# Four junctions of a two-block transformer on one core: last phases in threes, another order of the norm's chain, first products that take high parts by fours

## The chip, the core and the metric

One Trainium2 chip, one of its cores. The metric is the device time of one launch in microseconds, the median of several runs, for the whole network below. In the profile PE is TensorE, DVE VectorE, ACT ScalarE, POOL GpSimd, SP the queue that issues the weights' DMAs.

## What is computed

One sequence of 256 tokens, width 1024, float32. The first block has two layers, each a mixer and a SwiGLU FFN with adaptive modulation; the second block has a mixer (MoBA and gMLP), cross-attention to a memory and a PEER expert layer. What matters here is the step from one projection to the next norm, four times in the first block:

```python
mod = silu(c) @ ada_w + ada_b                       # shifts, scales, gates
y = concat(mixer outputs) @ w_out                   # or (silu(h@w_gate) * (h@w_up)) @ w_down
x = x + gate * rmsnorm(y, post_g)
h = rmsnorm(x, pre_g) * (1 + scale) + shift         # not modulated for the second block's mixer
# second mixer, from its input projection:
log_a = log_sigmoid((h @ w_glr) @ w_gk2 + b_gk) / 16
q, k = h @ w_gq, h @ w_gk                           # then GLA in chunks, v, gates, NSA
```

## The kernel before

All products in full precision are made of three: each f32 operand is cut into a high part (what the array's reduced format holds) and a low part (the rest), and high by high, high by low and low by high are summed in PSUM. Of the rows, hH and hL are high and low parts; of the weights, `whi` and `wlo`.

**Weights.** `weight_order` (L152) lists all slabs of 2048 columns in the order of their use. SP loads slab n into one of three places of `raw` once both low parts of slab n - 3 are made (L3250 to L3257). A slab has two blocks of 1024 columns. ACT makes a block's high part (`cut_hi`, L2489), and may do so as soon as the block three before it is used up, because `whi` and `wlo` are rings of three blocks. DVE, or POOL for blocks that `lo_engine` gives it, subtracts to get the low part (`cut_lo`, L1399). TensorE waits for the low part once, at a block's first tile (`tile`). How far ahead ACT and DVE cut is written into each stage (`se_cuts` and `ve_cuts`: two blocks past the last tile named). Each engine follows one list, so a cut asked for late in the list comes late.

**The modulation** of later stages is summed on DVE in pieces between other work (`ve_ada`, L1425 and L1428: two steps a piece, one 512 KB DMA each through a ring of two). After the fourth piece of a group TensorE turns the sum by eight matmuls (`pe_ada`, L742), and that call waits for the piece before it.

**A junction.** The last projection of a stage (`pe_out` for the mixers, `pe_down` 9 and 10 for the FFNs) accumulates four PSUM banks (two token tiles by two halves of the width). Its last phase takes the last two blocks (512 columns of moving operand, three products a tile) bank by bank, so that the banks end one after another. Ahead of it the gains of the gate are turned into rows (`pe_gate_rows`, L687) once DVE has made them (L1538). Then, by bank: ACT squares it (L2531), takes Ln and Exp for the root (L2542, L2544); DVE scales it (L1546) and updates x (L1555); ACT squares x and takes the root; DVE makes the unit rows (L1483); TensorE transposes them (L675), with fillers ahead so that it isn't idle (L669, L658; counts in `KEEP`). `se_junction` and `ve_junction` hold the order. From the transposes ACT makes high parts (L2603, L2601) and some shifted rows (L2607), DVE the other shifted rows (L1507) and the low parts (L1514, L1497) (`se_normed`, `ve_normed`). The first products of the next projection (`split` set) go tile by tile, and each waits for the high and the low part of its rows (`pe_split`). In the second FFN gate and up projections take high and low rows in one instruction of 512 columns (L582, `pe_linear_halves`).

**The second mixer's start** (`pe_mix1`, `ve_mix1`, `se_mix1`): w_glr, w_gqk 0, log_a (L1007), w_gqk 1 to 3. DVE adds the bias (L1919), ACT makes Abs, Exp and Ln (L2822, L2824, L2827) with two high parts between, DVE finishes (L1925, L1928) and scans (L1932). Then GLA begins (L1026).

Of the kernel before, what the change touches and what calls it, by code (L numbers as in the profile page):

```python
# [41 lines left out]
KEEP = {"ffn0": (16, 3, 8), "mix1": (16, 3, 8), "ffn1": (14, 3, 8), "mix2": (16, 3, 0), "peer": (0, 8, 0)}  # L42
# [14 lines left out]
FIRST = (("w_glr", 0, 0), ("w_mqk", 0, 0))  # L57
BY_PE = (2, 3, 6, 7)
SHIFTED_BY_ACT = (0, 2)
# [99 lines left out]
def weight_order():  # L159
# [19 lines left out]
    for name, n in (("w_glr", 1), ("w_gqk", 4), ("w_gv", 4), ("w_gg", 4), ("w_ncd", 1), ("w_nq", 2), ("cmp_w1", 2),  # L179
                    ("w_nks", 1)):  # L180
        some(name, *range(n))
# [21 lines left out]
class Weights:  # L203
# [3 lines left out]
    def __init__(self, counts, D, raw, whi, wlo, slots):  # L207
        self.counts, self.D, self.raw, self.whi, self.wlo, self.slots = counts, D, raw, whi, wlo, slots
        self.slabs = weight_order()
# [21 lines left out]
        half_slab("peer_up", 127)  # L231

# [13 lines left out]
    def lo_engine(self, j):  # L246
        name, i, half = self.blocks[j]
        if name[:6] in ("w_gate", "w_up0", "w_up1", "w_down"):
# [3 lines left out]
        return "G" if (name, i, half) in FIRST else "V"  # L252

    def parts(self, j):
# [3 lines left out]
        k = (j % NBLK) * BLK  # L258
        return w[:, half * BLK:half * BLK + cols], self.whi[:, k:k + cols], self.wlo[:, k:k + cols], ready
# [25 lines left out]
class Memory:  # L285


    def __init__(self, sb):
# [15 lines left out]
        self.hT = tiles8(self.hT_t)  # L304
        self.cs_parts, self.cs_pick = chi[0:48, 0:T], chi[0:48, T:T + 16]
# [162 lines left out]
def program(nc, D, out_dram):  # L468
    with ExitStack() as ctx:
# [21 lines left out]
        W = Weights(counts, D, m.raw, m.whi, m.wlo, [sem(f"slab_landed{k}") for k in range(NRAW)])  # L491
# [29 lines left out]
class Net:  # L521
# [70 lines left out]
    def pe_linear(self, e, name, i, kt, nn, xh, xl, split=None, eager=False, ada=True):  # L592
# [5 lines left out]
        order = [(j, k) for k in range(kt) for j in range(nn)] if split else [(j, k) for j in range(nn) for k in range(kt)]  # L598
        for n, (j, k) in enumerate(order):
            if eager and 2 * n == len(order):  # L600
                self.pe_ada(e)
            if split and j == 0:
                self.pe_split(e, split, k)
            keys = [("full", name, i)] if n == len(order) - 1 else []
            self.pe_mm3(e, ps[:, j * 256:(j + 1) * 256], self.W.tile(e, name, (i * nn + j) * kt + k), xh[:, k, :],
                        xl[:, k, :], n == 0 if split else k == 0, k == kt - 1, *keys)

    def pe_linear_halves(self, e, name, i, split=None):
# [3 lines left out]
        if split:  # L612
            for j in range(2):
                self.banks.take(e, name, i, j)
        for n in range(16):
            j, k = (n % 2, n // 2) if split else (n // 8, n % 8)
            if split and j == 0:
                self.pe_split(e, split, k)
            if not split and k == 0:
                self.banks.take(e, name, i, j)  # L620
# [86 lines left out]
    def pe_out(self, e, name, ks, xh, xl, first, last, nm, split=None, ada=True):  # L707
# [4 lines left out]
        for k in ks:  # L712
# [4 lines left out]
            if last and k >= ks[-1] - 1:  # L717
                continue
# [2782 lines left out]
```

## Time and profile before

| | us |
|---|---|
| median of 3 runs | 1981.6 (1979.27 to 1986.51) |
| the profiled execution | 1974.73 |
| its span, first to last instruction | 1972.9 |
| PE busy | 1887.3 (96%) |
| DVE busy | 1445.0 (73%) |
| ACT busy | 993.6 (50%) |
| POOL busy | 258.3 (13%) |

Busy time counts each engine's own instructions; a matmul's end is modelled, so two in a row overlap in the rows. A row of a timeline gives the start, the time, engine, line, tiles and, in brackets, how long the engine was idle before it and what released it. Rows that merge several like instructions say x2 or more; their time runs from the first start to the last end.

### The profile page before, as it was taken

The numbers are of one execution on the slowest core, as the hardware profiler recorded it, in microseconds if no ns is written. First come the engines' busy times: TensorE is split into PE (matmuls) and PEld (weight loads), VectorE is DVE, ScalarE is ACT, GpSimd is POOL, SyncE is SP. The second block draws the span as 40 slices with busy tenths as digits, with TensorE's granted clock in tenths as the row PEclk, the third lists the DMA queues.
The fourth block names the chain that finished last, engine by engine and source line by source line (L and its number), as shares of the span: only waits on it lengthen the run. The fifth ranks groups of instructions, "written<-read, shape, count | busy, mean of one in ns | idle before, by whom it ended". The sixth has DMA issues, their size and how long they took to land.

```text
span 1972.9 us, 31980 instructions
## 1 busy us (share of the span) xinstructions
PE 1887.3 (96%) x12506; PEld 1702.2 (86%) x12506; DVE 1445.0 (73%) x2618; ACT 993.6 (50%) x1442; POOL 258.3 (13%) x118
## 2 busy tenths in 40 slices
PE   6899899999989899999999899999999999999998
PEld 6887799989968788889898799999988888888886
DVE  5998775558957785557666559888878887777776
ACT  6645544455435544454555546566643334444444
POOL 0001044430001044430000175000000000000000
PEclk9999999999999999999999999999999999999999
DMA  8754476756464255546344344577767766465452
GB/s 327 246 185 151 146 269 250 260 203 225 169 233 146 99 206 188 191 151 231 137 150 171 125 153 172 191 215 215 214 209 260 299 235 232 174 235 192 176 207 108
DMA packets 94549, 391.88 MB, mean 199 GB/s; under 512 B 7680, under 2 KB 41776, under 8 KB 56000
## 3 DMA queue, kind: packets, MB, share of 16 engines
q1 hardware_dynamic: 94112, 389.58, 55.8%
q8 instruction: 100, 1.64, 0.3%
q10 hardware_dynamic: 288, 0.26, 0.1%
q14 instruction: 49, 0.40, 0.1%
HBM read 371.72 MB, written 15.73 MB: 196 GB/s over the span
## 4 chain that ended last, share of the span: by engine, by line
PE 76%; DVE 12%; ACT 3%; issue 2%; DMA 1%; POOL 0%; ACTq 0%; DVEq 0%; SPq 0%
PE ps L582 9%; PE acc L566 9%; PE acc L568 9%; PE acc L567 9%; PE ps L570 6%; PE ps L572 6%; PE ps L571 6%; PE ps L583 5%; PE acc L570 3%; PE acc L571 3%; PE acc L572 3%; DVE wlo L1399 2%; PE ps L1354 1%; PE acc L1354 1%; DVE arena L1428 1%
## 5 line engine op out<-in xcount | busy, mean ns | idle before, releaser
L2489 ACT ACTIVATE whi<-raw 128x1024 fp32r<-128x1024 f32 x557 | 588.4, 1059 | 450.2 <-PE acc L568 222.9
L1399 DVE TENSOR_TENSOR wlo<-raw,whi 128x1024 fp32r<-128x1024 f32 x461 | 560.9, 1224 | 282.0 <-ACT whi L2489 278.8
L570 PE MATMUL ps<-hpair,whi 128*128 128x256 f32 x1104 | 318.2, 288 | 10.5 <-DVE wlo L1399 6.3
L1399 POOL TENSOR_TENSOR wlo<-raw,whi 128x1024 fp32r<-128x1024 f32 x96 | 241.1, 2514 | 607.3 <-ACT whi L2489 607.0
L572 PE MATMUL ps<-hpair,wlo 128*128 128x256 f32 x1104 | 313.1, 284 | 0.0
L571 PE MATMUL ps<-hpair,whi 128*128 128x256 f32 x1104 | 313.0, 284 | 0.0
L566 PE MATMUL acc<-whi,chi 128*128 128x512 f32 x752 | 297.4, 395 | 3.5 <-DVE wlo L1399 1.9
L568 PE MATMUL acc<-wlo,chi 128*128 128x512 f32 x752 | 294.9, 392 | 0.0
L567 PE MATMUL acc<-whi,clo 128*128 128x512 f32 x752 | 294.2, 391 | 0.0
L582 PE MATMUL ps<-hpair,whi 128*128 128x512 f32 x800 | 284.8, 398 | 0.8 <-DVE hpair L1514 0.8
L570 PEld LDWEIGHTS ps<-hpair,whi 128*128 128x128 f32 x1104 | 212.4, 192 | 15.1 <-issue 4.9
L583 PE MATMUL ps<-hpair,wlo 128*128 128x256 f32 x800 | 224.5, 281 | 0.0
L571 PEld LDWEIGHTS ps<-hpair,whi 128*128 128x128 f32 x1104 | 212.5, 192 | 0.3
L572 PEld LDWEIGHTS ps<-hpair,wlo 128*128 128x128 f32 x1104 | 212.3, 192 | 0.0
L570 PE MATMUL acc<-hpair,whi 128*128 128x256 f32 x616 | 178.5, 290 | 7.2 <-ACT hpair L2603 4.2
L582 PEld LDWEIGHTS ps<-hpair,whi 128*128 128x128 f32 x800 | 150.3, 188 | 37.3 <-ACT hpair L2603 1.0
L572 PE MATMUL acc<-hpair,wlo 128*128 128x256 f32 x616 | 175.0, 284 | 0.0
L571 PE MATMUL acc<-hpair,whi 128*128 128x256 f32 x616 | 175.0, 284 | 0.0
L566 PEld LDWEIGHTS acc<-whi,chi 128*128 128x128 f32 x752 | 141.9, 189 | 35.1 <-issue 2.9
L568 PEld LDWEIGHTS acc<-wlo,chi 128*128 128x128 f32 x752 | 141.7, 188 | 31.9
L567 PEld LDWEIGHTS acc<-whi,clo 128*128 128x128 f32 x752 | 142.0, 189 | 27.4
L583 PEld LDWEIGHTS ps<-hpair,wlo 128*128 128x128 f32 x800 | 151.1, 189 | 2.5
(458 smaller groups left out, 2950.7 us busy)
## 6 DMA issues: line engine op xcount, KB each, us to landing
raw<-in_peer_down SPq DMA_DIRECT2D x64, 1024.0 KB, 4.9
raw<-in_peer_up SPq DMA_DIRECT2D x64, 1024.0 KB, 5.0
arena<-in_ada SPq DMA_DIRECT2D x80, 512.0 KB, 4.8
raw<-in_w_gate SPq DMA_DIRECT2D x22, 1024.0 KB, 4.7
raw<-in_w_up SPq DMA_DIRECT2D x22, 1024.0 KB, 4.8
raw<-in_w_down SPq DMA_DIRECT2D x22, 1024.0 KB, 4.8
arena<-spill SPq DMA_DIRECT2D x14, 1024.0 KB, 6.8
spill<-hT_t SPq DMA_DIRECT2D x22, 448.0 KB, 6.1
```

The lines of the kernel that those rows point to most:

```text
L566: e.matmul(out, xh, hi, start=start, stop=False, skip_group_check=True)
L567: e.matmul(out, xl, hi, start=False, stop=False, skip_group_check=True)
L568: i = e.matmul(out, xh, lo, start=False, stop=stop, skip_group_check=True)
L570: e.matmul(out, hi, xh, start=start, stop=False, skip_group_check=True)
L571: e.matmul(out, hi, xl, start=False, stop=False, skip_group_check=True)
L572: i = e.matmul(out, lo, xh, start=False, stop=stop, skip_group_check=True)
L582: e.matmul(ps.rearrange("p (s t) -> p s t", s=2), hi, self.m.hP[:, k], start=k == 0, stop=False, skip_group_check=True)
L583: i = e.matmul(ps[:, 0:T], lo, self.m.hH[:, k, :], start=False, stop=k == 7, skip_group_check=True)
L1354: t = e.matmul(ps[:, i * 128:(i + 1) * 128], m.oh1[:, n % 3, i * 128:(i + 1) * 128], m.oh2[n % 3][:, i * 128:(i + 1) * 128], start=True, s ...
L1399: e.tensor_tensor(out=lo, in0=w, in1=hi.bitcast(F32), op=ALU.subtract).then_inc(*X(("lo", j)))
L1428: e.scalar_tensor_tensor(out=m.ada_acc, in0=w, scalar=c, in1=m.ada_acc, op0=ALU.mult, op1=ALU.add).then_inc(*V(*([("ada", s)] if k else [])))
L2489: e.activation(hi, w, ACT.Copy, scale=1.0).then_inc(*self.A(("hi", j)))
```

## The change

- `SPARE`: the last block of w_out0b, w_down0, w_out1b and w_down1 gets a place of its own, half of `chi` and `clo`, outside the rings, so that four blocks can be live. The last phase of the four projections takes three blocks instead of two (`tail=3`; in `pe_down` the second half of call 9 moves into call 10, behind the gate rows).
- `se_junction`: the cut of a weight block moves behind the last root; one square over a whole row of the first token tile replaces two, with eps from a constant. `ve_junction`: the eps steps move to match.
- `pe_first`, for all first products: four rows' high parts, then their low parts, and the second block's low part last. `lo_engine`: that second block's low part is POOL's in `FIRST` (gate 0, gate 1, w_gqk 0, w_mqk 0), and DVE's cut inside `ve_normed` goes.
- `ve_normed`, `se_normed`: the shifted rows of pair 0 are DVE's now. `KEEP`: fewer fillers.
- Second mixer: w_gqk 0 before w_glr, log_a after w_gqk 1.

```diff
-KEEP = {"ffn0": (16, 3, 8), "mix1": (16, 3, 8), "ffn1": (14, 3, 8), "mix2": (16, 3, 0), "peer": (0, 8, 0)}
+KEEP = {"ffn0": (13, 2, 2), "mix1": (13, 2, 2), "ffn1": (12, 2, 2), "mix2": (13, 2, 0), "peer": (0, 8, 0)}
-FIRST = (("w_glr", 0, 0), ("w_mqk", 0, 0))
+FIRST = (("w_gate0", 0, 1), ("w_gqk", 0, 1), ("w_gate1", 0, 1), ("w_mqk", 0, 1))
+SPARE = {("w_out0b", 1, 1): ("used", "w_out0a"), ("w_down0", 10, 1): ("end", "mixer0", "P"),
+         ("w_out1b", 1, 1): ("used", "w_out1a"), ("w_down1", 10, 1): ("end", "mixer1", "P")}
-SHIFTED_BY_ACT = (0, 2)
+SHIFTED_BY_ACT = (2,)
...
+    def pe_first(self, e, name, i, kt, outs, starts, xh, xl, split, full):
+        nn = len(outs)
+        for k0 in range(0, kt, 4):
+            for k in range(k0, k0 + 4):
+                e.wait_ge(*self.at("hi", split, k))
+                for j in range(nn):
+                    if j == 0:
+                        hi, lo, _ = self.W.tile(e, name, i * nn * kt + k)
+                    else:
+                        b, hi = self.W.high(name, (i * nn + j) * kt + k)
+                        if k == 0:
+                            e.wait_ge(*self.at("hi", b))
+                    e.matmul(outs[j][0], hi, xh[:, k, :], start=k == 0 and j in starts, stop=False, skip_group_check=True)
+                    if j == 0:
+                        e.matmul(outs[0][0], lo, xh[:, k, :], start=False, stop=False, skip_group_check=True)
+            for k in range(k0, k0 + 4):
+                e.wait_ge(*self.at("lo", split, k))
+                for j in range(nn):
+                    t = e.matmul(outs[j][1], self.W.high(name, (i * nn + j) * kt + k)[1], xl[:, k, :], start=False,
+                                 stop=j == 0 and k == kt - 1, skip_group_check=True)
...
+        for j in range(1, nn):
+            for k in range(kt):
+                _, lo, end = self.W.tile(e, name, (i * nn + j) * kt + k)
+                t = e.matmul(outs[j][0], lo, xh[:, k, :], start=False, stop=k == kt - 1, skip_group_check=True)
...
-        for n in range(8):
-            tt, half, kk = (n // 4, n // 2 % 2, n % 2) if i == 10 else (n // 2 % 2, n % 2, n // 4)
+        order = ([(tt, half, k) for tt in range(2) for half in range(2) for k in (19, 20, 21)] if i == 10 else
+                 [(tt, half, 2 * i + kk) for kk in range(1 if i == 9 else 2) for tt in range(2) for half in range(2)])
...
     def pe_mix1(self, e):
-        self.pe_linear(e, "w_glr", 0, 8, 1, m.hH, m.hL, "mix1")
         for i in range(4):
-            self.pe_linear(e, "w_gqk", i, 8, 2, m.hH, m.hL)
+            self.pe_linear(e, "w_gqk", i, 8, 2, m.hH, m.hL, None if i else "mix1")
             if i == 0:
+                self.pe_linear(e, "w_glr", 0, 8, 1, m.hH, m.hL)
+            elif i == 1:
                 e.wait_ge(self.landed["gk2"], 16)
...
     def ve_normed(...):
         whole(1)
-        if first:
-            self.cut_lo(e, V, self.W.last(first, 0) + 1)
+        e.wait_ge(*self.at("hi", nm, 1))
+        whole(0)
         low(0)
...
     def ve_junction(...):
         self.ve_scaled(e, post, 1, 0)
-        self.ve_eps(e, norm, 0, 48)
         self.ve_scaled(e, post, 1, 1)
         self.ve_update(e, post, 1, 0)
         self.ve_update(e, post, 1, 1)
+        self.ve_eps(e, norm, 1, 48)
         self.ve_unit(e, norm, 0, self.m.x)
-        self.ve_eps(e, norm, 1, 48)
         self.ve_unit(e, norm, 1, self.m.x)
...
     def ve_mix1(...):
             self.ve_linear(e, "w_gqk", i, 8, 2, ada=i != 1)
             if i == 0:
+                self.ve_linear(e, "w_glr", 0, 8, 1)
+                e.wait_ge(*self.at("full", "w_glr", 0))
+                e.tensor_copy(m.low, self.banks.tile("w_glr", 0)[0:56, 0:T]).then_inc(*V(("out", "w_glr", 0)))
+            elif i == 1:
                 for h0 in range(0, 4, 2):     # additions, then ve_ada, ve_cuts(e, "w_gqk", 31), log_gate: as before
...
     def se_junction(...):
         self.se_acc_square(e, post, 1, 0)
-        self.cut_hi(e, self.W.last(first, 0) + 1)
-        self.se_x_square(e, norm, post, 0, 0)
+        self.se_row_square(e, norm, post, 0, 48)
         self.se_acc_square(e, post, 1, 1)
         self.se_root(e, post, 1, 56)
-        self.se_x_square(e, norm, post, 0, 1)
-        self.se_root(e, norm, 0, 48)
+        self.se_root(e, norm, 0, 48, self.m.kc("eps"))
         self.se_x_square(e, norm, post, 1, 0)
         self.se_x_square(e, norm, post, 1, 1)
         self.se_root(e, norm, 1, 48)
+        self.cut_hi(e, self.W.last(first, 0) + 1)
...
     def se_mix1(...):
+                self.se_linear(e, "w_glr", 0, 8, 1)
+            elif i == 1:
                 e.preload_act_table_set(LOG_SET)
...
                 e.activation(m.bcum, m.bcum, ACT.Exp, scale=-1.0).then_inc(*A())
-                self.se_cuts(e, "w_gqk", 31)
+                self.se_cuts(e, "w_gqk", 47)
...
     def ge_mix1(...):
-        self.cut_lo(e, self.G, self.W.last("w_glr", 0) + 2)
-        self.ge_cuts(e, "w_glr", 7)
+        self.cut_lo(e, self.G, self.W.last("w_gqk", 0) + 2)
```

## Rows read from the trace of the kernel before

**Rows 1.** The page: busy time, share of the span and instructions of each engine.

```profile
PE 1887.3 (96%) x12506; PEld 1702.2 (86%) x12506; DVE 1445.0 (73%) x2618; ACT 993.6 (50%) x1442; POOL 258.3 (13%) x118
```

**Rows 2.** Timeline, TensorE, first junction: start, us, engine, line, tiles [idle before <- releaser].

```profile
217.64 0.48 PE L566 MATMUL acc<-whi,hpair 128*128 128x512 f32 x1
...
224.09 0.50 PE L566 MATMUL acc<-whi,hpair 128*128 128x512 f32 x1 [0.73 <-DVE wlo L1399]
...
230.12 3.73 PE L669 MATMUL ps<-kc_t 128*128 128x128 f32 x32
```

**Rows 3.** Timeline, VectorE, first junction.

```profile
221.36 1.54 DVE L1428 SCALAR_TENSOR_TENSOR arena<-arena,gs_t 128x512 f32<-128x512 f32 x2 [1.52 <-DMA arena<-in_ada]
222.81 3.49 DVE L1399 TENSOR_TENSOR wlo<-raw,whi 128x1024 fp32r<-128x1024 f32 x3
```

**Rows 4.** Timeline, ScalarE, first junction.

```profile
229.69 1.06 ACT L2489 ACTIVATE whi<-raw 128x1024 fp32r<-128x1024 f32 x1
...
231.27 0.58 ACT L2531 ACTIVATE arena<-acc 128x512 f32<-128x512 f32 x1
...
237.00 1.02 ACT L2603 ACTIVATE hpair<-ps,mod_t,gs_t 128x256 fp32r<-128x256 f32 x2 [1.11 <-PE ps L675]
```

**Rows 5.** Timeline, first junction: DVE's last low part, next block's first product.

```profile
242.62 0.69 DVE L1514 TENSOR_TENSOR hpair<-hT_t,hpair 128x512 fp32r<-128x512 f32 x1 [0.16 <-ACT hpair L2603]
...
246.61 0.36 PE L570 MATMUL ps<-hpair,whi 128*128 128x256 f32 x1
```

**Rows 6.** Timeline, second junction: VectorE, TensorE, ScalarE.

```profile
426.02 0.17 DVE L1538 TENSOR_TENSOR gs_t<-mod_t,pv_t 128x8 f32<-128x8 f32 x1
...
433.95 3.73 PE L669 MATMUL ps<-kc_t 128*128 128x128 f32 x32
...
435.46 0.58 ACT L2531 ACTIVATE arena<-acc 128x512 f32<-128x512 f32 x1
...
440.77 1.02 ACT L2603 ACTIVATE hpair<-ps,mod_t,gs_t 128x256 fp32r<-128x256 f32 x2 [1.11 <-PE ps L675]
```

**Rows 7.** Timeline, TensorE, second mixer's start.

```profile
453.86 1.99 PE L1007 MATMUL acc<-arena 16*128 16x256 f32 x8
...
461.64 1.05 PE L742 MATMUL ps<-kc_t,arena 128*128 128x128 f32 x8
...
469.14 0.36 PE L570 MATMUL ps<-hpair,whi 128*128 128x256 f32 x1 [0.69 <-ACT arena L2501]
...
475.81 2.05 PE L1026 MATMUL acc<-arena 128*128 128x128 f32 x16 [0.69 <-ACT arena L2501]
```

**Rows 8.** Timeline, VectorE and ScalarE, second mixer's start.

```profile
456.87 1.54 DVE L1428 SCALAR_TENSOR_TENSOR arena<-arena,gs_t 128x512 f32<-128x512 f32 x2
...
460.88 1.15 ACT L2827 ACTIVATE arena<-arena,kc_t 128x1024 f32<-128x1024 f32 x1
...
464.19 2.44 DVE L1932 TENSOR_TENSOR_SCAN arena<-arena 128x256 f32<-128x256 f32 x4
...
467.78 2.35 DVE L1399 TENSOR_TENSOR wlo<-raw,whi 128x1024 fp32r<-128x1024 f32 x2
```

**Rows 9.** Timeline, VectorE, third junction.

```profile
671.33 1.22 DVE L1399 TENSOR_TENSOR wlo<-raw,whi 128x1024 fp32r<-128x1024 f32 x1
```

**Rows 10.** Timeline, VectorE and TensorE, fourth junction.

```profile
868.51 2.12 DVE L1876 TENSOR_TENSOR clo<-arena,chi 128x512 fp32r<-128x512 f32 x1 [0.70 <-ACT chi L2800]
...
872.02 1.09 PE L687 MATMUL ps<-kc_t,gs_t 128*128 128x128 f32 x8 [0.23 <-DVE gs_t L1538]
...
878.43 3.73 PE L669 MATMUL ps<-kc_t 128*128 128x128 f32 x32
...
892.13 1.23 DVE L1399 TENSOR_TENSOR wlo<-raw,whi 128x1024 fp32r<-128x1024 f32 x1 [2.84 <-DMA arena<-in_sin]
```

**Rows 11.** Stretches: us, PE busy (x), granted clock (1.00 is 2.4 GHz), DMA, GB/s.

```profile
554.40:558.80 4.40, 4.37 (x11) 0.50 0.89 328
```

**Rows 12.** Timeline, TensorE, first product of the experts' queries.

```profile
1128.46 0.38 PE L570 MATMUL ps<-hpair,whi 128*128 128x256 f32 x1 [1.18 <-DVE hpair L1497]
```

More of the change, by code:

```diff
@@ L178, in weight_order @@
     ffn(0)
-    for name, n in (("w_glr", 1), ("w_gqk", 4), ("w_gv", 4), ("w_gg", 4), ("w_ncd", 1), ("w_nq", 2), ("cmp_w1", 2),
+    some("w_gqk", 0)
+    some("w_glr", 0)
+    some("w_gqk", 1, 2, 3)
+    for name, n in (("w_gv", 4), ("w_gg", 4), ("w_ncd", 1), ("w_nq", 2), ("cmp_w1", 2),
                     ("w_nks", 1)):
@@ L231, in __init__ @@
         half_slab("peer_up", 127)
+        self.turn, self.owner = [], []
+        for j, key in enumerate(self.blocks):
+            self.turn.append(len(self.owner))
+            if key not in SPARE:
+                self.owner.append(j)
     def begin(self):
@@ L2534, in se_square, with se_row_square, se_root @@
         self.junk_written[k] = self.A.last
-    def se_root(self, e, nm, tt, at):
+    def se_row_square(self, e, nm, src, tt, at):
+        m = self.m
+        for half in range(2):
+            e.wait_ge(*self.at("x", src, tt, half))
+            if self.squares_made > 1:
+                e.wait_ge(*self.junk_written[half])
+        e.activation(m.junk, m.x[:, tt, :], ACT.Square, scale=1.0 / 32.0,
+                     accum_out=m.small[:, at + 2 + tt:at + 3 + tt]).then_inc(*self.A(("square", nm, tt, 1)))
+        self.junk_written = [self.A.last, self.A.last]
+    def se_root(self, e, nm, tt, at, eps=None):
         m, A = self.m, self.A
@@ L2594, in se_normed @@
             e.wait_ge(*self.at("full", nm, "turned", jj))
-            if shifts is not None and jj not in SHIFTED_BY_ACT:
+            if shifts is not None and jj in SHIFTED_BY_ACT:
+                for j in (2 * jj, 2 * jj + 1):
+                    e.activation(out[:, j, :], ps[:, (j % 2) * 256:(j % 2) * 256 + T], ACT.Identity,
+                                 bias=shifts[:, j:j + 1], scale=gains[:, j:j + 1]).then_inc(*A(("whole", nm, j)))
+            elif shifts is not None and jj:
                 e.wait_ge(*self.at("whole", nm, 2 * jj + 1))
@@ L2598, in se_normed @@
                 src = ps[:, (j % 2) * 256:(j % 2) * 256 + T]
-                last = j % 2 and shifts is not None and jj not in SHIFTED_BY_ACT
                 if shifts is None:
@@ L2603, in se_normed @@
                     e.activation(H[:, j, :], src, ACT.Identity, bias=shifts[:, j:j + 1], scale=gains[:, j:j + 1]).then_inc(
-                        *A(("hi", nm, j), *([("out", nm, "turned", jj)] if last else [])))
-            if shifts is not None and jj in SHIFTED_BY_ACT:
-                for j in (2 * jj, 2 * jj + 1):
-                    e.activation(out[:, j, :], ps[:, (j % 2) * 256:(j % 2) * 256 + T], ACT.Identity,
-                                 bias=shifts[:, j:j + 1], scale=gains[:, j:j + 1]).then_inc(
-                                     *A(("whole", nm, j), *([("out", nm, "turned", jj)] if j % 2 else [])))
+                        *A(("hi", nm, j)))
         if first:
```

104 lines of the change are left out of this document (64 added, 40 removed).

## The prediction

> **What bounds the kernel now.** I read the page first, then the engines' timelines around the four junctions (after the out-projection of either mixer and after either FFN). The page: TensorE is busy for 96% of the span [rows 1], so an edit counts by the idle time it takes from TensorE or adds to it, and by nothing else. At a junction the last product of the old projection is followed by fillers (230.12), then there is a chain ACT, DVE, TensorE up to the first high part of the normed rows (237.00), then the first products [rows 2, 4]. I call the fillers' start E and that high part's start T1. E to T1 is 6.9 us at the first junction and 6.8 at the second [rows 2, 4, 6]; by the same two views it is 6.5 at the third and 6.7 at the fourth. The prize is small. The risk sits in what feeds the stretches on either side of it: weights' low parts on DVE, and a log-gate chain after the second junction.
>
> **Last phase in threes.** No product is added. The phase that finishes the four accumulators takes 36 products (0.23 us each: 24 of them and eight small transposes fill 872.02 to 878.43 [rows 10]), so the work that may run before it shrinks by 12 products, 2.7 us. The spare block lets the high parts of the last block be made early, but what comes late is on DVE:
> - First junction. TensorE starts the projection at 217.64. Its first block takes 2.8 us, the second block's share for one accumulator 0.7, so the third block's low part is wanted at 221.1. DVE makes it at 222.8, behind a copy of modulation weights that waits for its DMA (1.52 us) [rows 3], and nothing in the change moves that. Today the same block is wanted after 24 products, and costs 0.73 [rows 2]. The third block starts at 224.09 as now, the fourth at 225.2, and 27 products follow: E at 232.1 instead of 230.1, **+2.0**, with 3.0 us of idle.
> - Second. The rows of gate gains are turned before the last phase, and want DVE's product of 426.02 [rows 6]. With one block less ahead TensorE is there at 424.9 and waits until 426.25. From there eight transposes and 36 products take 6.4 + 2.7: E at 435.3 instead of 433.95, **+1.4**.
> - Third. Low parts three and four come from DVE at 671.33 and 1.2 us later [rows 9], 0.3 and 0.5 us late for the new order: **+0.8**.
> - Fourth. The same wait is already open: the rows start at 872.02, 0.23 us after DVE's product. DVE was held by a low part of the activation that took 2.12 us [rows 10]. They can't start earlier, and 12 more products lie behind them: **+2.7**, with 3.1 us of idle before.
>
> Together +6.9. Bounds: 0, if the low parts were on time everywhere, and 12 products four times, 11.
>
> **The chain's order.** ACT no longer makes a weight block's high part inside the chain (229.69, 1.06 us) nor a square of the first half before the last accumulator's. At the first junction that square began 1.15 us after E [rows 2, 4]; now I take 0.2, the semaphore's way to an engine that is free. From it to T1 it was 5.7, and 5.3 at the second, where no GpSimd instruction ran beside the x updates (435.46 to 440.77) [rows 4, 6]. The new order has that case everywhere: GpSimd gets its block only after ACT's last root. One square over a whole row replaces two, and is done before the last accumulator. So E to T1 is 0.2 + 5.3 = 5.5: **-1.4, -1.3, -1.0, -1.2**, together -4.9. Bounds: -6 and -3, by a filler or wait of half a us at each. Fewer fillers cost nothing: 13 of 0.23 us end before the first transposes may start at E + 3.5.
>
> **First products by fours.** They may start on high parts alone, 2 us sooner. But they end with the low parts: DVE has one more pair of shifts to do, so its last low part ends 6.4 us after T1 where it ends 6.3 now (242.62 + 0.69) [rows 5]. The last four of the rows' low products and the eight with the second block's low part follow, some 8.0 after T1 instead of 8.8; then the next block waits for DVE's modulation piece and low part, 9.3 instead of 9.6 (246.61) [rows 5]. **-0.3** at the first junction, 0 at the third, within -1 and +1.
>
> The second block's low part is now GpSimd's: 2.4 us where DVE took 1.2. At the fourth junction it releases the slab that the SP queue waits for, behind which the loads of cos and sin stand; DVE waits for sin until 892.13 [rows 10] before it makes the third block's low part. That comes 1.2 us later after T1: **+1.2**, bounds 0 and 1.5.
>
> The port: the activation's low part took 2.12 us, as all do here that begin while GpSimd subtracts [rows 10]. The Trainium skill, SBUF — State Buffer, "Who interferes with whom", says that a VectorE instruction with two SBUF inputs and a GpSimd one that reads SBUF exclude each other for the whole instruction; the trace agrees. By that rule the first low part of the rows may wait some 0.3 us for GpSimd's block, 1.2 over four junctions; by the sum above, nothing.
>
> The input projection of the first stage is bound by DVE's low parts, 0. Before the experts' queries TensorE waits 1.18 us for a low part that four high parts can now precede [rows 12]; with the memory keys' projection, which waits likewise, **-1.5**, between -2.5 and 0.
>
> **The order in the second mixer.** This is where I put the weight. Now: w_glr, w_gqk 0, log_a (453.86), w_gqk 1, a modulation transpose (461.64), w_gqk 2, w_gqk 3 (469.14), first GLA product (475.81) [rows 7]. After: w_gqk 0, w_glr, w_gqk 1, log_a, the rest. So log_a starts later and the chain behind it has one projection less to hide in. On DVE the low parts of w_gqk 3 come only after log_gate and the scans, since the cut asked for before them stays at tile 31 and is already made. In times after T1 (440.77 now):
> - w_gqk 0 ends at 8.0; w_glr's low part is ready at 9.2 (piece 1.5, block 1.2, after 6.4), w_glr 2.9, w_gqk 1 5.8: log_a at 18.0, now 13.1.
> - DVE's additions and its piece end 4.55 after log_a's start (456.87 + 1.54) [rows 8]: 22.55. The modulation transpose in front of w_gqk 2 needs that piece. Today it is ready three us before; then TensorE idles 2.7 us, and w_gqk 2 runs from 23.4 to 29.2.
> - ACT must make both blocks of w_gqk 3 before its Ln (1.15 us [rows 8]); the second waits for w_gqk 2's first half, 26.4. Ln ends at 28.7, DVE's two steps and scans take 4.6 from there (462.03 to 466.63), the next piece 1.15 (to 467.78) [rows 8], the low part 1.2: 35.6.
> - w_gqk 3 at 35.8 instead of 28.4 [rows 7]. **+7.4**, with 6.5 us of idle.
>
> DVE and ACT go in step with TensorE there, by the blocks' release, so the 4.61 us of idle before 554.43 won't shrink. Bounds: 0, if DVE got ahead, and 9.
>
> **Clock.** After the idle of 4.61 us TensorE ran 4.4 us at a granted clock of 0.50 [rows 11], the 1.2 GHz level, half of which is lost. After 6.5 us of idle I expect the same: **+2.4** (0 to 3.4). Of idle times of three us I have no plain case and take 0, though each could cost 1.7, the same half of a stretch three quarters as long.
>
> **Sum.** 6.9 - 4.9 - 0.3 + 1.2 - 1.5 + 7.4 + 2.4 = +11.2 us. The profiled execution had 1974.7 us (span 1972.9), so 1986; the median of three is 6.9 higher, 1981.6, and I add the same to it: **1993 us**, +0.57%.
>
> **Rivals.**
> - *The junctions do what the edits suggest*, and neither low parts nor log_a stand in the way: -4.9 from the chain, -0.9 for the waits of today at the first junction, -0.8 from first products at three junctions, -1.5 further on: about -9, **1973**. For it: the spare block does free ACT earlier, and lateness of 0.3 to 0.5 us, as at the third, is what a queue may give back. Against it: gate gains are late today already (872.02) [rows 10], and DVE is behind a DMA at 221.36 [rows 3]. It decides only if the log chain as well begins its scans 7 us sooner than I have it.
> - *The log chain hides*, the rest as computed: 11.2 - 7.4 - 2.4 = +1.4, **1983**. For it: w_gqk 3's wait is short now (467.78 + 1.2 is 469.0, it starts at 469.14) [rows 7, 8]. Against it: it waits at all, so nothing is spare.
> - *Every stall drops the clock*: the four of 1.4 to 3.1 us cost up to 1.7 each, three of them deciding, +5: **1998**. It decides once the array idles three us.
>
> **Numbers.** Forecast 0.46, junctions gain 0.12, log chain hidden 0.27, clock everywhere 0.15. What a measurement can tell from no change is 0.5%, 9.9 us. The forecast and the last rival lie above +9.9 with some spread down, the second rival is the same, the first splits between same and faster: slower 0.51, same 0.39, faster 0.10. Range 1974 to 2001; the forecast's own is 1988 to 1999.
>
> **What would show it.** In the profile after: idle of about 3 us within the out-projection and before the gate rows of the second FFN; E to T1 of 5.5; first products within 1 us of T1; about 2.7 us before the modulation transpose and 6.5 before w_gqk 3; a stretch at 0.50 behind that. It is wrong if w_gqk 3 starts under 30 us after T1, or if E comes no later after the projection's start than now.

## The result, and the profile after

| | before | after |
|---|---|---|
| median of four runs each, us | 1981.6 (1979.3 to 1986.5) | 2001.8 (2000.4 to 2002.4) |
| profiled execution, us (span) | 1974.7 (1972.9) | 2002.4 (2000.6) |
| mean granted clock in the profile | 0.991 | 0.986 |

The change makes the kernel slower: ratio 1.0106, 95% interval 1.0091 to 1.0120, +20.2 us. The forecast was 1993, the range 1974 to 2001: the direction was right, the size half, and the time lies just outside. Between the two profiled executions lie 27.7 us, since the one of before ran 6.9 us under its median; 2.7 of them pass before the kernel's first transposes, where nothing was changed. The mean granted clock over the four runs after is 0.984.

The page after has TensorE busy for 95% of a longer span, with three more busy microseconds than [rows 1]:

```profile
PE 1890.6 (95%) x12456; PEld 1704.2 (85%) x12456; DVE 1447.7 (72%) x2621; ACT 991.6 (50%) x1426; POOL 260.9 (13%) x119
```

TensorE's timeline where the rows of before stood: the third block of the first out-projection [rows 2], E and the first product of the first junction [rows 2], the gate rows of the second [rows 6], the modulation transpose, w_gqk 3 and the first GLA product [rows 7], the gate rows of the fourth [rows 10], and w_mqk 1 behind it.

```profile
226.47 0.79 PE L596 MATMUL acc<-whi,hpair 128*128 128x512 f32 x1 [2.90 <-DVE wlo L1467]
235.59 3.06 PE L733 MATMUL ps<-kc_t 128*128 128x128 f32 x26
244.07 0.39 PE L656 MATMUL ps<-hpair,whi 128*128 128x256 f32 x1 [1.91 <-DVE hpair L1580]
...
432.38 1.09 PE L751 MATMUL ps<-kc_t,gs_t 128*128 128x128 f32 x8 [3.20 <-DVE gs_t L1605]
441.50 3.06 PE L733 MATMUL ps<-kc_t 128*128 128x128 f32 x26
447.85 0.36 PE L656 MATMUL acc<-hpair,whi 128*128 128x256 f32 x1
...
469.64 2.08 PE L806 MATMUL ps<-kc_t,arena 128*128 128x128 f32 x8 [2.61 <-DVE arena L1496]
485.57 0.55 PE L600 MATMUL ps<-hpair,whi 128*128 128x256 f32 x1 [6.44 <-DVE wlo L1467]
493.79 0.38 PE L1094 MATMUL acc<-arena 128*128 128x128 f32 x1 [0.69 <-ACT arena L2569]
...
894.27 1.09 PE L751 MATMUL ps<-kc_t,gs_t 128*128 128x128 f32 x8 [2.92 <-DVE gs_t L1605]
922.01 0.36 PE L600 MATMUL ps<-hpair,whi 128*128 128x256 f32 x1 [3.72 <-DVE wlo L1467]
```

These are six stalls of 2.6 us and more where there was none. Two further ones grew in a part that wasn't changed: 3.16 us at 610.93 (before 1.72) and 3.28 at 643.66 (before 1.65). The stall of 4.6 us that ended at 554.43 is still there as well. Around the end of five of the six, the view by stretches (columns: the stretch, its length, busy time and instructions of PE, PE's weight loads, DVE, ACT and POOL, then the granted clock, the DMA share, GB/s):

```profile
226.20:229.60 3.40, 3.13 (x7) 2.44 (x8) 2.49 (x3) 0.17 (x1) 0.00 (x0) 0.51 0.44 120
468.60:475.40 6.80, 5.76 (x27) 5.76 (x28) 0.95 (x2) 2.44 (x3) 0.00 (x0) 0.50 0.61 229
482.20:489.00 6.80, 3.43 (x16) 3.46 (x17) 6.62 (x10) 0.00 (x0) 0.00 (x0) 0.50 0.43 124
895.20:898.60 3.40, 3.40 (x11) 2.66 (x10) 0.16 (x1) 3.18 (x4) 0.00 (x0) 0.51 0.91 306
922.60:926.00 3.40, 3.40 (x19) 3.40 (x18) 1.54 (x2) 0.00 (x0) 0.00 (x0) 0.51 0.91 326
```

Where the 27.7 us arise, from the starts of the same work in both traces: 2.7 before the first stage, 0.4 of them won back before the first junction; E later behind the gate rows by 3.2, 2.8, 0.9 and 4.3, and the second gate rows themselves 0.6 later, because TensorE waits for them; E to T1 shorter by 1.3, 1.2, 0.9 and 1.2; T1 of the second junction to the first GLA product 46.7 instead of 35.0, +11.7; from there to the third junction +4.4; from the fourth T1 through w_mqk +4.7; the memory keys -1.1; behind the experts' queries -1.5. The last term can't be put down to the change: from that T1 to the end it is 846.2 us before and 844.7 after, but also 844.8 in b_fills below, which has no part of the change.

### The profile page after: what moved, and what is told of

Read it like the earlier page. It is cut to its first block, busy times and chain, and to the rows that moved or that the text cites. A ratio compares the mean times of both kernels' runs of the same rounds, so it can differ in the third digit from the quotient of the medians.

```text
span 2000.6 us, 31805 instructions
## 1 busy us (share of the span) xinstructions
PE 1890.6 (95%) x12456; PEld 1704.2 (85%) x12456; DVE 1447.7 (72%) x2621; ACT 991.6 (50%) x1426; POOL 260.9 (13%) x119
## 4 chain that ended last, share of the span: by engine, by line
PE 76%; DVE 14%; ACT 2%; issue 2%; DMA 1%; POOL 0%; ACTq 0%; DVEq 0%; SPq 0%
PE ps L612 9%; PE acc L596 9%; PE acc L598 9%; PE acc L597 9%; PE ps L600 5%; PE ps L602 5%; PE ps L601 5%; PE ps L613 5%; PE acc L600 3%; PE acc L601 3%; PE acc L602 3%; DVE wlo L1467 2%; DVE arena L1496 2%; PE ps L1422 1%; PE acc L1422 1%
## 5 line engine op out<-in xcount | busy, mean ns | idle before, releaser
L600 PE MATMUL ps<-hpair,whi 128*128 128x256 f32 x1024 | 296.7, 290 | 16.0 <-DVE wlo L1467 16.0
L601 PE MATMUL ps<-hpair,whi 128*128 128x256 f32 x1024 | 291.8, 285 | 0.0
L602 PE MATMUL ps<-hpair,wlo 128*128 128x256 f32 x1024 | 291.7, 285 | 0.0
L612 PE MATMUL ps<-hpair,whi 128*128 128x512 f32 x784 | 279.0, 398 | 0.0
L613 PE MATMUL ps<-hpair,wlo 128*128 128x256 f32 x784 | 219.9, 281 | 0.0
L600 PEld LDWEIGHTS ps<-hpair,whi 128*128 128x128 f32 x1024 | 198.6, 194 | 19.3 <-DVE wlo L1467 11.1
L601 PEld LDWEIGHTS ps<-hpair,whi 128*128 128x128 f32 x1024 | 198.7, 194 | 0.3
L602 PEld LDWEIGHTS ps<-hpair,wlo 128*128 128x128 f32 x1024 | 198.5, 194 | 0.0
L612 PEld LDWEIGHTS ps<-hpair,whi 128*128 128x128 f32 x784 | 147.3, 188 | 35.6
L600 PE MATMUL acc<-hpair,whi 128*128 128x256 f32 x600 | 173.0, 288 | 3.2 <-DVE wlo L1467 2.6
L602 PE MATMUL acc<-hpair,wlo 128*128 128x256 f32 x600 | 169.7, 283 | 0.0
L601 PE MATMUL acc<-hpair,whi 128*128 128x256 f32 x600 | 169.6, 283 | 0.0
L613 PEld LDWEIGHTS ps<-hpair,wlo 128*128 128x128 f32 x784 | 147.9, 189 | 2.5
```

Source lines behind the costliest of these rows:

```text
L600: e.matmul(out, hi, xh, start=start, stop=False, skip_group_check=True)
L601: e.matmul(out, hi, xl, start=False, stop=False, skip_group_check=True)
L602: i = e.matmul(out, lo, xh, start=False, stop=stop, skip_group_check=True)
L612: e.matmul(ps.rearrange("p (s t) -> p s t", s=2), hi, self.m.hP[:, k], start=k == 0, stop=False, skip_group_check=True)
L613: i = e.matmul(ps[:, 0:T], lo, self.m.hH[:, k, :], start=False, stop=k == 7, skip_group_check=True)
```

## The experiments

T1, E and "first product" are used as in the prediction. Each kernel was timed in five rounds beside the kernel before on its own chip, so ratios are what compares them; the changed kernel's own is 1.0106, and 0.0010 is 2 us. Each ratio has an interval of some 0.0014 either way, so the difference of two ratios is uncertain by about 4 us. It is less, about 2 us, for a_mixold, a_mixold_twos and a_mixold_fills, which ran side by side on one chip.

**a_mixold.** The second mixer's order undone:

```diff
-    some("w_gqk", 0); some("w_glr", 0); some("w_gqk", 1, 2, 3)
+    some("w_glr", 0); some("w_gqk", 0, 1, 2, 3)          # and the four engines' lists of before
```

> The changed kernel with one part undone: the second mixer begins with w_glr, then w_gqk 0, log_a, w_gqk 1 to 3, as before. Everything else of the change stays. In the profiles the stretch from T1 of the second junction to the first GLA product went from 35.0 to 46.7 us. Theory A, the new order costs exactly this stretch (two waits of 2.6 and 6.4 us and two stretches of half clock behind them): 11.7 us come back, the time is 1990 us, against 2001.8 of the changed kernel. Theory B, part of it was hidden later anyway (the decays of the GLA stage follow the scans whatever TensorE does): 7.4 or less comes back, 1994 or more. Theory C, the modulation transfers behind (3.2 us of idle at 610.93 where there were 1.7) hang on it as well: 15 come back, 1987.

1994.1 us, 1.0073 (1.0060 to 1.0086): 6.5 us back. By the number this is theory B (7.4 or less), but not for its reason: the stretch itself didn't return to what it was. T1 to the first GLA product became 39.5 us, not 35.0. TensorE's and DVE's timelines show why:

```profile
454.48 0.55 PE L597 MATMUL acc<-hpair,whi 128*128 128x256 f32 x1 [2.40 <-DVE wlo L1463]
```

```profile
450.83 0.69 DVE L1576 TENSOR_TENSOR hpair<-hT_t,hpair 128x512 fp32r<-128x512 f32 x1 [0.55 <-ACT hpair L2681]
451.66 1.54 DVE L1492 SCALAR_TENSOR_TENSOR arena<-arena,gs_t 128x512 f32<-128x512 f32 x2
453.12 2.35 DVE L1463 TENSOR_TENSOR wlo<-raw,whi 128x1024 fp32r<-128x1024 f32 x2
```

w_glr has one block, and what follows it, w_gqk 0, had its low part made by DVE inside the norm before. The change took that cut out; it now comes behind the last low part of the rows and a piece of modulation. Between 453.3 and 460.1 the clock was 0.50. So the mixer's new order belongs to the new first product: undoing it alone is no clean undo.

**a_mixold_cut** moves that cut ahead of the piece:

```diff
+        self.cut_lo(e, V, self.W.last("w_glr", 0) + 1)
         self.ve_linear(e, "w_glr", 0, 8, 1)
```

> The changed kernel with the old order in the second mixer, as in the run a_mixold, and the low part of w_gqk 0's first block moved ahead of the piece of modulation on DVE. In a_mixold that low part began 1.5 us later than it could, TensorE idled 2.4 us before w_gqk 0 (454.48) and ran 6.8 us at half clock behind it: log_a came 17.5 us after T1, as late as in the changed kernel, where it had been 13.1. Theory A, the first product by fours with its block handed to GpSimd only works where the first projection has two blocks, and that cost most of what undoing the order gave back: 5.4 us less than a_mixold, ratio 1.0046. Theory B, the half clock or DVE finds another place: 2.4 less or nothing.

1991.0 us, 1.0050 (1.0034 to 1.0066), 4.6 less than a_mixold by the ratios; idle before w_gqk 0 is 0.72 us, log_a comes 14.9 us after T1 and the first GLA product 36.8. Theory A. Against the changed kernel (1.0106) this cleaner undo gives 11 us back, close to the 11.7 that the traces show for the second mixer's start.

**b_order.** The chain's order alone, in the kernel before:

```diff
-        self.cut_hi(e, self.W.last(first, 0) + 1)
-        self.se_x_square(e, norm, post, 0, 0)
+        self.se_row_square(e, norm, post, 0, 48)       # and the rest of both junction lists
```

> The kernel before with one part of the change alone: the order of the chain at the four junctions (row squares in one instruction, no high part and no eps step of the norm inside the chain), last phases still in twos, old filler counts, old first products, old mixer order. My prediction's term: E to T1 falls by 1.4, 1.3, 1.0 and 1.2, together -4.9, so 1976.7 us (ratio 0.9975). Rival: with the last accumulator only 1.4 us behind the one before it (2.1 with threes), the whole-row square of the first half no longer fits ahead of it, and the high part of the first block now comes after the roots, so that the first product waits for it: E to T1 near 6.3 and the first product later, -1 or nothing.

1985.8 us, 1.0035 (1.0019 to 1.0051): slower, by 7, where I had -4.9. E to T1 in its trace is 7.2, 9.0, 7.2 and 9.0 us. ScalarE at the second junction, where E is 440.77:

```profile
442.39 1.06 ACT L2542 ACTIVATE arena<-x_t 128x1024 f32<-128x1024 f32 x1 [1.58 <-DVE small L1474]
443.63 0.60 ACT L2530 ACTIVATE arena<-acc 128x512 f32<-128x512 f32 x1
```

The whole-row square needs both updated halves of x, and in twos these aren't there when the last accumulator is: its square (443.63) begins 2.9 us after E instead of 0.2. In threes the accumulators end 2.1 us apart and the row's square fits between. The rival I wrote named this; its size was still too small. The term -4.9 is a gain of two parts together. Not all of the 7 us is the chain, though. E to T1 grew by 5.5 us over the four junctions, with TensorE idle for 2.59 us before the transposes of the second and the fourth and a stretch at 0.50 behind each. And in this trace a modulation transfer landed 2.7 us later than in [rows 3]: DVE waited 4.25 us for it, and E came 4.0 us later behind the first gate rows. Whether the other runs had that too, no trace shows.

**a_mixold_twos.** Last phases in twos in a_mixold:

```diff
-        self.pe_out(e, "w_out0b", range(4), m.hH, m.hL, False, True, "mix0_post", tail=3)
+        self.pe_out(e, "w_out0b", range(4), m.hH, m.hL, False, True, "mix0_post")   # SPARE = {}
```

> The changed kernel with the old order in the second mixer and with last phases in twos again (no spare block); left of the change are the chain's order, the first products by fours and the new filler counts. The trace of the changed kernel has E later after the projection's start by 3.2, 3.4, 0.9 and 4.3 us at the four junctions, 11.8 together. Theory A, that is the price of the threes: 11.8 less than with the old mixer order alone, about 1978. Theory B, the threes are what lets E to T1 be 5.5: it goes back to 6.3 or so, and 3 of the 11.8 stay, about 1981.

1991.0 us, 1.0061 (1.0049 to 1.0073), 2.4 less than a_mixold by the ratios, not 11.8. Gate rows to E is as before (13.4, 6.3, 11.8, 6.4), but E to T1 is 6.9, 9.7, 8.2 and 9.6. Theory B, and more of it than I had: with this order and these filler counts threes cost 2 us net, just clear of noise, and without them the order doesn't work. The kernel keeps the changed kernel's smaller filler counts, and TensorE idled 3.25 and 3.40 us before the transposes of the second and the fourth junction, at 0.50 behind both; b_order, with the old counts, has 2.0 us less of E to T1 in all. Twos with the old counts were not run, so the price of the threes alone isn't known from this pair. First products by fours were never undone alone either.

**a_mixold_fills** and **a_fills2** ask what a stall costs in clock. Both put fillers ahead of waits and shorten none:

```diff
+        self.pe_spend(e, 11)                     # products of ones into the bank that is next in turn
         e.wait_ge(*self.at("gate_g", nm))
```

> The changed kernel with the old order in the second mixer, and fillers in the idle time of some 3 us within the last phases: 22 ahead of the third block of the first out-projection, 24 and 22 ahead of the turned gate gains of the first and second FFN. They fill time in which TensorE waits anyway and move nothing. Theory A, an idle time of 3 us is what drops the granted clock (0.50 for 3.4 us at 226.2 and at 895.2): with the fillers it stays at 1.00 there, E comes 1.2 and 1.5 us earlier, 2.7 less than without them. Theory B, the clock falls for another reason, or the fillers end later than the wait: no change against the kernel without them, or 1 more.

1990.2 us, 1.0056 (1.0044 to 1.0068), 3.4 less than a_mixold. The stretches at 0.50 at 224.5 and 886.7 are gone from the trace, but this run doesn't show what that is worth. Its fillers were twice as long as I reckoned (0.23 us each, 22 of them 5.1 us) and ended up to 2 us after the waits, so that from the first T1 to the second its trace is 1.9 us longer than a_mixold's. What the trace wins, 5.5 us, lies between the first GLA product and the third junction, where it has no filler. The counts were put right for the next:

> The changed kernel with nothing but fillers added, each 0.23 us, in five idle times that the change made, some 0.3 to 0.6 us fewer than the idle time: 11 before the third block of the first out-projection (idle 2.9 us in the trace), 11 before the turned gate gains of either FFN (3.2 and 2.9), 10 before the modulation transpose and 25 before w_gqk 3 in the second mixer (2.6 and 6.4). No wait gets shorter. Theory A, an idle time of 2.6 us or more is what drops the granted clock: the stretches at 0.50 from 226.2, 468.6, 482.2 and 895.2 go away, in which TensorE did 2.5, 5.8, 3.4 and 3.0 us of work at half pace; half of that, 7.4 us, comes back: ratio to before 1.007 where the changed kernel had 1.0106. Theory B, the granted clock follows something else: 1.0106 stays, and the stretches too.

1993.3 us, 1.0064 (1.0050 to 1.0079): 8.3 us back, give or take 4, against 7.4 worked out. The same places in its trace:

```profile
225.00:228.40 3.40, 2.91 (x16) 2.05 (x16) 3.40 (x4) 0.05 (x1) 0.00 (x0) 1.00 0.61 214
466.00:482.50 16.50, 15.46 (x132) 15.11 (x132) 9.80 (x15) 6.83 (x7) 0.00 (x0) 1.00 0.32 113
482.50:489.00 6.50, 5.81 (x49) 5.61 (x49) 5.42 (x7) 1.94 (x3) 0.00 (x0) 1.00 0.84 295
888.00:892.00 4.00, 3.85 (x21) 3.34 (x22) 0.10 (x1) 3.13 (x4) 0.00 (x0) 1.00 0.67 229
```

Theory A. Up to T1 at the first junction the trace is 1.2 us shorter than the changed kernel's behind the gate rows, 4.1 from the second T1 to the first GLA product and 1.0 from the third T1 to the fourth: 6.3 us at the places that were filled. The mean granted clock over the runs is 0.989, where the changed kernel has 0.984. So a third or more of the loss of 20 us was clock, lost behind stalls, while the waits themselves stayed as long as they were.

**a_logfix.** One argument on DVE in the second mixer:

```diff
-                self.ve_cuts(e, "w_gqk", 31)
+                self.ve_cuts(e, "w_gqk", 47)
                 e.wait_ge(*self.at("log_gate"))
```

> The changed kernel with one argument changed: the low parts that DVE makes ahead of its wait for the log gate in the second mixer reach to w_gqk 3's last block (tile 47 where it was 31). Theory A, w_gqk 3 then starts right behind w_gqk 2 (no idle of 6.4 us, no half clock behind it), the scans end 2.4 us earlier relative to T1 and have slack before the GLA levels want them: 8 us or more come back, ratio 1.0065. Theory B, DVE's chain of levels, 85 to 95% busy behind the scans, sets the pace there, so what TensorE wins before its first GLA product it loses waiting for factors (the idle time of 4.6 us before the states grows): 3 or less comes back, ratio 1.009 or more.

1993.7 us, 1.0062 (1.0048 to 1.0076), 8.7 back. TensorE's first GLA product and DVE:

```profile
484.01 2.05 PE L1094 MATMUL acc<-arena 128*128 128x128 f32 x16 [0.69 <-ACT arena L2569]
```

```profile
475.88 1.23 DVE L1467 TENSOR_TENSOR wlo<-raw,whi 128x1024 fp32r<-128x1024 f32 x1 [5.07 <-ACT whi L2557]
479.06 2.44 DVE L1999 TENSOR_TENSOR_SCAN arena<-arena 128x256 f32<-128x256 f32 x4
```

The low part is made before the scans, there is no wait ahead of w_gqk 3, and the first GLA product comes 38.5 us after T1 (445.56) instead of 46.7. Behind it 1.6 us are lost again (idle at 493.38 where there was none), and the 4.6 us before the states stay 4.6. Theory A, with a small piece of B.

**a_early.** Two moves on DVE for the threes:

```diff
+            if k == 2 and name[-1] == "b":       # ve_out: low parts ahead of the second piece
+                self.cut_lo(e, self.V, self.W.last(name, 7, 512))
...
+            if i == 10:                          # ve_ffn: ahead of the last activation's low part
+                self.ve_gate_rows(e, f"ffn{layer}_post", layer, 5, f"g_ffn_post{layer}")
```

> The changed kernel with two small moves on DVE that repair what the last phase in threes found late: in the out-projections' second halves the low parts of all four blocks come ahead of the second piece of modulation (which waits for its DMA), and in the FFNs the product that makes the gate gains comes ahead of the last activation's low part, where no GpSimd subtraction runs beside it. Theory A, the threes were dear only by these: idle of 2.9, 3.2 and 2.9 us at the first, second and fourth junction falls under 1 us each, and the half clock at 226.2 and 895.2 goes: -3.2, -3.0, -4.3, some 10 us, ratio 1.0055. Theory B, twelve more products behind the last wait are lost anyway since something else is as late (the spare block's low part, ACT's turned gains): -4, ratio 1.0085.

1990.5 us, 1.0049 (1.0035 to 1.0062), 11.3 back. Theory A. Gate rows to E at the first junction is 12.3 us, where it was 16.6 after and 13.3 before; the gate rows of the second and the fourth wait 0 and 1.06 us. What the move did to one instruction stands in DVE's timeline; first the changed kernel, with GpSimd's subtraction beside it, then this one:

```profile
429.86 2.44 POOL L1467 TENSOR_TENSOR clo<-raw,chi 128x1024 fp32r<-128x1024 f32 x1 [2.68 <-ACT chi L2557]
430.14 2.19 DVE L1605 TENSOR_TENSOR gs_t<-mod_t,pv_t 128x8 f32<-128x8 f32 x1
```

```profile
422.23 0.17 DVE L1607 TENSOR_TENSOR gs_t<-mod_t,pv_t 128x8 f32<-128x8 f32 x1
```

**a_bank.** The first product of each FFN in accumulator banks:

```diff
+            self.banks.order = ROT if i else ACC[1:3]
```

> The changed kernel with the first product of each FFN in accumulator banks 1 and 2 (free at that point) instead of the next bank in turn, which is the one the turned rows stand in and which DVE's first low part frees. Theory A, that bank's release is why the first product began 2.9 us after T1 at the first junction and 3.6 at the third, but 0.8 at the second, where eight banks are in turn: now 0.8 at all three. The product still ends with the low parts, so what follows it comes at most 1.0 us earlier at the first junction and 1.2 at the third; ratio 1.0095 to 1.0106. Theory B, it waits for DVE's low part for another reason: the first product stays at 2.9 and 3.6.

2002.8 us, 1.0101 (1.0086 to 1.0117), no change that can be measured. The first products begin 0.76 and 0.82 us after T1 at the first and third junction:

```profile
241.07 0.36 PE L656 MATMUL acc<-hpair,whi 128*128 128x256 f32 x1
248.24 1.16 PE L806 MATMUL ps<-kc_t,arena 128*128 128x128 f32 x8
249.47 0.35 PE L600 MATMUL ps<-hpair,whi 128*128 128x256 f32 x1
```

Theory A. The next projection (249.47) starts 9.2 us after T1 where it was 9.6: an early start is given back at the low parts.

**a_repaired** joins a_early, a_logfix and the wait for cos and sin put where they are first used:

```diff
-        for name in ("cos2", "sin2"):
-            e.wait_ge(self.landed[name], 16)
         for i in range(4):
             self.ve_linear(e, "w_mqk", i, 8, 2)
+            if i == 2:
+                for name in ("cos2", "sin2"):
+                    e.wait_ge(self.landed[name], 16)
```

> The changed kernel with four repairs of order on DVE, nothing computed otherwise: the two moves of a_early, the argument of a_logfix, and in the second block's first mixer the wait for the transfers of cos and sin put ahead of the first rope instead of ahead of the weights' low parts. In the changed kernel's trace that wait held DVE for 6.05 us until 920.64, TensorE idled 3.7 us (922.01) and then ran 3.4 us at half clock. Theory A, the parts add: 11.3 (a_early against the changed kernel), 8.7 (a_logfix), 4.9 (the last), so 2000.9 - 24.9 = 1976 on this chip's scale, ratio 0.998, the first version with the change in it that is no slower than before. Theory B, they share what they win (the half clock after one stall moves to the next): ratio 1.002 or more.

The wait that it moves, in the changed kernel's DVE timeline:

```profile
920.64 3.50 DVE L1467 TENSOR_TENSOR wlo<-raw,whi 128x1024 fp32r<-128x1024 f32 x3 [6.05 <-DMA arena<-in_sin]
```

1977.6 us, 0.9982 (0.9973 to 0.9991): 24.5 us back against 24.9 forecast, theory A. Two of the three parts of that forecast were measured (11.3 and 8.7); the third, 4.9 for the wait for cos and sin, was worked out and never run alone. So that the parts add is borne out only together with that estimate; from the fourth T1 to the experts' T1 the trace is 5.5 us shorter than the changed kernel's.

**b_fills** and **a_repaired_fills** put fillers into stalls that were left: b_fills at three places of the kernel before, a_repaired_fills at the same three, ahead of the GLA outputs, and before the second mixer's modulation transpose, a stall that only the change made.

> The kernel before, without any part of the change, with fillers of 0.23 us in its own idle times: 17 before the first query heads (4.7 us), 17 before the compression's hidden layer (4.6), 5 before the first turned probabilities (1.7), and with the later wait for cos and sin. Theory A, the stretches at half clock from 139.0 and 552.0 (6.8 us each, all of it but the first 0.5 to 2.4 us under work) go: 5 to 6 us less, with 0.5 for the later wait, ratio 0.997. That tells how much of a_repaired_fills is the clock alone, and owes nothing to the change. Theory B, the clock falls at the next idle time instead: 1.000.

1975.2 us, 0.9964 (0.9951 to 0.9978), at a mean granted clock of 0.994 over its runs.

> a_repaired with fillers of 0.23 us in idle times that stay: 10 before the modulation transpose of the second mixer (2.6 us idle), 17 before the first query heads (4.7), 17 before the compression's hidden layer in the GLA stage (4.6), 8 before the piece of modulation ahead of the GLA outputs (1.7 or 3.1), 10 before the first turned probabilities of the selected attention (3.3). Theory A, each of these drops the granted clock today for 3.4 or 6.8 us and TensorE works through most of it: 2.6, 3, 3, 1.6 and 1 us come back, 11 in all, ratio 0.993. Theory B, the fillers end late in two of the places (the idle time there is shorter in this kernel), and half of it is lost again: ratio 0.996.

1967.1 us, 0.9927 (0.9914 to 0.9940), the fastest version, 14 us under the kernel before. Its mean granted clock over the runs is 0.996, where the kernel before beside it has 0.991. Its page has a clock of 0.9 or more in every slice; so has the page of the kernel before, while the changed kernel's has two slices at 0.8, so this row alone shows no gain over before:

```profile
PE   6999899999999899999999899999999999999998
...
PEclk9999999999999999999999999999999999999999
```

Both theories A. How the 14 us divide depends on the order in which one counts: fillers give 7 us in the kernel before (with them the later wait for cos and sin, forecast at 0.5), the mended change without fillers gives 4, and fillers at five places instead of three give 11 on top of it.

## Why the prediction failed, step by step

- *Last phase in threes, +6.9.* Measured +11.8 by the traces: 3.2, 3.4, 0.9 and 4.3 from the projection's start to E, where I had 2.0, 1.4, 0.8 and 2.7. The places were right, and so were the idle times at the first and the fourth junction (2.9 and 2.9 us where I had 3.0 and 3.1); the third junction was exact. Two things were missed. At the second junction TensorE idled 3.2 us and not 1.4. There the gate gains' product was priced at its usual 0.17 us; it took 2.19, since it now began while GpSimd subtracted the spare block (429.86, 2.44 us). I had seen that lock in [rows 10] and taken the port at nothing. The Trainium skill, SBUF — State Buffer, "Who interferes with whom", says that a VectorE instruction with two SBUF inputs contends with a GpSimd one that reads SBUF, over a port pair that is an exclusive lock; the trace agrees: the product ended with the subtraction, and a_early shows the other side, 0.17. And the clock fell behind two of the stalls, 1.3 and 1.5 us.
- *Chain's order, -4.9.* -4.6 by the traces, E to T1 5.5 to 5.6 at all four: right in place and size, wrong as a term of its own. b_order gives +7 for it alone, 5.5 of that in E to T1. I argued "0.2 to an engine that is free" from the order with threes and wrote it as a gain of the order.
- *First products by fours, -0.3 and 0, beginning within 1 us of T1.* The next projection starts 9.58 us after T1 at the first junction (9.61 before), so the small term was right or near it; the sign that I named was wrong at three of four junctions: 2.9, 0.8, 3.6 and 1.8 us. At the FFNs four banks are in turn, the first product takes one in which the turned rows stand, and DVE's first low part now releases it (L1580); I had followed the parts and not the bank. At the fourth DVE's first low part is again what ends the wait (1.18 us, 1.22 before).
- *Slab release at the fourth junction, +1.2.* Measured +4.7, 1.5 of it clock. The chain of causes was the predicted one (SP's loads wait for GpSimd's low part); but sin landed 7.0 us after its issue, not 5.0, DVE waited 6.05 us (before 2.84, [rows 10]), TensorE 3.7, and the clock fell. If the repairs add, a_repaired leaves 4.6 us for this one, beside those of a_early and a_logfix.
- *Second mixer, +7.4, and its clock, +2.4.* Measured 11.7 where I had 9.8. log_a came 17.95 us after T1 (predicted 18.0), the idle times were 2.6 and 6.4 us (2.7 and 6.5): the mechanism and both waits were right. But the smaller stall dropped the clock too, for 6.8 us, 5.8 of them under work, and w_gqk 3 came at 38.5 instead of 35.8. The smaller stall's half clock cost 2.9, half of that work; the one behind the larger stall cost 1.6, not 2.4.
- *Clock, "idle times of three us I take at 0".* This is the step that failed: of the eight stalls between 2.6 and 3.8 us in the trace, seven drew a stretch at 0.50; only the 3.20 us at 432.38 did not. At the first and fourth junction, in the second mixer and in w_mqk such stretches cost 1.3, 1.5, 2.9 and 1.5 us, 7.2 that I had at nothing, and no other single step that failed is as large: the port cost 1.9, sin 2.0. My third rival had it, at +5 for four stalls and with a chance of 0.15; it would have given 1998 and was still short, by the port and by sin. a_fills2 gives 8.3 us back for the clock of four stalls, the one of 6.4 us among them, 6.3 by its trace. The Trainium skill, TensorE: Matmul & The Clock Gate, "HAM oscillation — how this bites in real kernels", describes it: waits for data in the middle of work, and the array at the low clock after each; the trace agrees at those seven, the shortest of them 2.61 us. I had gone by one row only, [rows 11], and it was not the only case. The trace of before has a plain one at the first stage's first product, TensorE's timeline and the stretch behind it:

```profile
39.02 0.35 PE L570 MATMUL acc<-hpair,whi 128*128 128x256 f32 x1 [3.46 <-ACT hpair L2603]
...
40.00:43.40 3.40, 3.40 (x18) 0.50 0.12 48
```

Idle of 3.46 us, then 3.4 us of full work at half clock, 1.7 lost: read beforehand, it would have put the "plain case" that the prediction says it lacks beside its four stalls.

- *Experts' queries and memory keys, -1.5.* The keys gave -1.1; the queries still wait 1.19 us (1.18 in [rows 12]), on DVE's low part (L1563), which frees the bank there as well.
- *From the first GLA product to the third junction* I predicted nothing; it became +4.4. A modulation transfer landed 1.4 us later (TensorE idle 3.16 at 610.93, before 1.72), then 3.4 us at half clock; further on TensorE idled 3.28 us at 643.66 (before 1.65), with 6.8 us at half clock. The four transfers issued there took SP 9.2 us in three of the fourteen traces (before, b_order, a_mixold_fills), 9.6 in a_repaired_fills and 10.4 to 11.1 in the other ten, b_fills among them, which has no part of the change. What decides it stays open: no part of the change divides the kernels that way.

The rivals: junctions gaining, whose terms sum to -8.1 and not the -9 written, didn't happen, but a_repaired shows what it wanted, DVE's low parts in time. The hidden log chain is what one argument would have bought.

## What to carry to other kernels

Price a stall of some 3 us twice, as idle time and as the half clock that may follow it (1.3 to 2.9 us here), and look for every such stall in the trace that you have; if the wait can't go, fill it with products into a free bank, and fill a little less than its length. When an edit makes a phase want its inputs earlier, list for every engine the instruction that makes each input and what is ahead of it in that engine's list: here four small moves in VectorE's list were worth 24.5 us and turned a loss of 1.1% into a gain of 0.2% (0.1 to 0.3). And don't book terms of parts that share a chain: run one alone before you trust it alone.

## What was not expected of the hardware

- Idle of 2.61 us dropped the clock in the second mixer in each kernel that had it, while idle of 3.20 us before the gate rows of the first FFN did not in the changed kernel, a_mixold, a_mixold_cut and a_logfix; in a_bank the same idle time did, for 6.8 us. In a_bank, in turn, 2.77 us at 226.66 and 2.92 us at 896.41 did not, where the changed kernel's 2.90 and 2.92 at the same places did. So near three us the length of a stall alone doesn't decide.
- A product of 128x8 held by a GpSimd subtraction takes thirteen times its time, 2.19 for 0.17 us.
- One profiled execution lay 6.9 us under the median of its kernel. Of the 27.7 us between two spans a quarter was no effect of the change.
